# Latent attention on one core: a head's output product moved behind the next head's scores

## The reference

```python
q = (_rms_norm(c_q, q_norm) @ w_q_up).reshape(B, L, H, QK_NOPE + QK_ROPE)   # 128 + 64 per head
q_nope, q_rope = q[..., :QK_NOPE], _rope(q[..., QK_NOPE:], pos)
kv = (_rms_norm(c_kv, kv_norm) @ w_kv_up).reshape(B, L, H, QK_NOPE + V_HEAD)
k_nope, v = kv[..., :QK_NOPE], kv[..., QK_NOPE:]
k_rope = _rope(k_rope, pos)                                                  # one for all heads
for s, e in bounds:                          # 0-16, then blocks of 128 queries
    sc = (q_nope[s:e] . k_nope[:e] + q_rope[s:e] . k_rope[:e]) * scale       # causal
    p = softmax(where(mask, sc, neg))
    outs.append(p @ v[:e])
o = concatenate(outs)
return (o * silu(g)) @ w_out                 # 2048 -> 1024
```

## Time and profile before

| what | value |
|---|---|
| median of three runs | 2272.62 us |
| profiled execution | 2278.24 us |
| its span | 2276.1 us |
| PE busy | 2119.0 us (93%) |
| DVE, ACT, POOL busy | 1245.8, 894.0, 910.9 us |
| the 16 heads (1370.6 to 1665.0 us) | 294.4 us, of which PE busy 281.7 us |
| mean granted clock of TensorE in the heads | 0.98 |

### The profile page before, as it was taken

How to read it: one execution, slowest core, us unless ns; L and a number is a source line. 1 busy time by engine, 2 the same in 40 slices (tenths; PEclk the granted TensorE clock), 3 DMA queues, 4 the chain that set the end, 5 groups by cost and what they waited for, 6 DMA issues and landing times.

```text
span 2276.1 us, 57765 instructions
## 1 busy us (share of the span) xinstructions
PE 2119.0 (93%) x23476; PEld 1799.1 (79%) x23476; DVE 1245.8 (55%) x2016; ACT 894.0 (39%) x2246; POOL 910.9 (40%) x592
## 2 busy tenths in 40 slices
PE   6999999989999999987989999999898999998997
PEld 4789999978888888875989957777698776776775
DVE  8766656665665666664046514545411475428674
ACT  1665555535655555555231123333323101302351
POOL 1132322333133233245437811232344598456455
PEclk8999999999999999997999999999899999999999
DMA  2334444474335334414212211010123221221102
GB/s 96 113 142 157 160 174 168 158 191 78 73 73 96 74 72 96 84 35 142 87 53 93 93 65 38 19 37 19 38 66 130 77 92 56 74 82 57 47 0 74
DMA packets 158991, 198.08 MB, mean 87 GB/s; under 512 B 121040, under 2 KB 123344, under 8 KB 156496
## 3 DMA queue, kind: packets, MB, share of 16 engines
q1 hardware_dynamic: 158800, 195.25, 28.2%
HBM read 156.24 MB, written 38.99 MB: 86 GB/s over the span
## 4 chain that ended last, share of the span: by engine, by line
PE 59%; issue 7%; DVE 5%; POOL 4%; ACT 2%; POOLq 1%; DVEq 0%; ACTq 0%
PE wide L922 9%; PE wide L1416 9%; PE wide L1417 9%; PE wide L1418 9%; PE wide L2059 5%; PE wide L2178 3%; PE wide L1947 2%; PE wide L2132 1%; PE wide L2771 1%; PE wide L2162 1%; PE wide L2451 1%; PE wide L2754 1%; POOL x_w L1221 1%; PE wide L947 1%; PE wide L2136 1%
## 5 line engine op out<-in xcount | busy, mean ns | idle before, releaser
L1416 PE MATMUL wide<-mixed_high,w_high_rwkv_in 128*128 128x264 f32 x880 | 255.1, 290 | 3.6 <-issue 2.1
L1418 PE MATMUL wide<-mixed_high,w_low_rwkv_in 128*128 128x264 f32 x880 | 250.5, 285 | 0.0
L1416 PEld LDWEIGHTS wide<-mixed_high,w_high_rwkv_in 128*128 128x128 f32 x880 | 166.5, 189 | 19.4 <-issue 13.0
L1221 POOL TENSOR_TENSOR x_w<-n,masks 128x192 f32<-128x192 f32 x48 | 28.6, 597 | 357.2 <-ACT n L1094 357.2
L1418 PEld LDWEIGHTS wide<-mixed_high,w_low_rwkv_in 128*128 128x128 f32 x880 | 166.4, 189 | 0.0
L1437 POOL TENSOR_TENSOR w_high<-weights,con 128x1024 fp32r<-128x1024 f32 x45 | 108.7, 2416 | 73.8 <-PE wide L1418 46.3
L644 POOL TENSOR_TENSOR w_low_rwkv_in<-weights,w_high_rwkv_in 128x1024 fp32r<-128x1024 f32 x29 | 70.5, 2431 | 143.9 <-ACT w_high_rwkv_in L477 143.9
L922 PE MATMUL wide<-x_w,n_levels 64*64 64x64 f32 x2752 | 121.4, 223 | 6.4 <-DVE x_w L1173 1.5
L922 PE MATMUL wide<-e,x_w 64*64 64x64 f32 x2752 | 120.2, 219 | 0.7 <-issue 0.7
L1158 DVE TENSOR_TENSOR b_and_k<-wide,b_k_masks 128x384 f32<-128x384 f32 (+1 forms) x160 | 75.3, 512 | 83.0 <-PE wide L982 83.0
L1440 POOL TENSOR_TENSOR w_low<-weights,w_high 128x1024 fp32r<-128x1024 f32 x45 | 118.5, 2632 | 3.5
(11 more groups left out here) (407 smaller groups left out, 6566.2 us busy)
## 6 DMA issues: line engine op xcount, KB each, us to landing
weights<-in_stream SPq DMA_DIRECT2D x200, 512.0 KB, 3.6
forms<-form SPq DMA_DIRECT2D x16, 2020.5 KB, 6.3
forms_in<-forms SPq DMA_DIRECT2D x96, 144.0 KB, 4.6
forms_in<-forms SPq DMA_DIRECT2D x32, 288.0 KB, 4.4
gate_bonus<-forms SPq DMA_DIRECT2D x16, 576.0 KB, 4.3
r_ahat_r<-forms SPq DMA_DIRECT2D x32, 144.0 KB, 3.6
mixed<-gate_bonus SPq DMA_DIRECT2D x14, 264.0 KB, 2.1
gated<-mixed SPq DMA_DIRECT2D x14, 264.0 KB, 4.8
```

The lines of the kernel that those rows point to most:

```text
L1416: pe.matmul(dst, w[0], x[0], start=start, stop=False)
L1418: return pe.matmul(dst, w[1], x[0], start=False, stop=stop)
```

## The change

In all four programs the output product and the gating of head H - 1 are done within head H. On PE, the output product of H - 1 (now the function `pe_output`) follows the scores of H and precedes the projections for H + 1. On DVE, its gating (now `dve_gate`) stands between `share(3)` and the second reciprocal. For head 15 the last output product and gating come at the end, as before.

Two orders within the projections change. When the next head is odd, q comes ahead of k on PE and ACT. When it is even, ACT copies the rotary part after all the exponentials. The wait before the turning moves with it: in front of an odd head it is for the copy of q (which is the fourth of the pair's five copies). The wait for two steps of the rotation, which stood before the output product, goes; the wait for all six steps stays before the scores. The first turn of `over_heads` is written out, and the loop runs the two turns behind it.

The diff:

```diff
--- before.py
+++ after.py
@@ -2066,28 +2066,30 @@
             if x % 2 == 0:
                 ring.wait_full(pe, k_load, j)
                 product(wide[2], wr, 0, Q_TILES).then_inc(e["made"], 1)
-            if not first:
-                pe.wait_ge(e["gated"], 2 * H)
-            mm = product(wide[3], wk, Q_TILES, KV_TILES)
-            mm.then_inc(e["made"] if x % 2 == 0 else ring.done(k_load), 1)
+            def keys():
+                if not first:
+                    pe.wait_ge(e["gated"], 2 * H)
+                mm = product(wide[3], wk, Q_TILES, KV_TILES)
+                mm.then_inc(e["made"] if x % 2 == 0 else ring.done(k_load), 1)
+            if x % 2 == 1:
+                product(wide[2], wq, 0, Q_TILES).then_inc(ring.done(q_load), 1)
+                keys()
+                return
+            keys()
+            ring.wait_full(pe, q_load, j)
             if first:
-                ring.wait_full(pe, q_load, j)
                 pe.wait_ge(e["evac"], 1)
                 for b in range(2):
                     mm = pe.matmul(wide[1][:, b, 0:HALF], mcon("rot_mla", P), q_rope_raw[:, b * HALF:(b + 1) * HALF], start=True, stop=True)
                 mm.then_inc(e["made"], 1)
                 product(wide[2], wq, 0, Q_TILES).then_inc(e["made"], 1)
                 return
-            if x % 2 == 0:
-                ring.wait_full(pe, q_load, j)
-                pe.wait_ge(e["evac"], 5 * pair + 1)
-            mm = product(wide[2], wq, 0, Q_TILES)
-            mm.then_inc(e["made"] if x % 2 == 0 else ring.done(q_load), 1)
-            if x % 2 == 0:
-                pe.wait_ge(e["evac"], 5 * pair + 2)
-                for b in range(2):
-                    mm = pe.matmul(wide[3][:, b, 0:HALF], mcon("rot_mla", P), q_rope_raw[:, b * HALF:(b + 1) * HALF], start=True, stop=True)
-                mm.then_inc(e["made"], 1)
+            pe.wait_ge(e["evac"], 5 * pair + 1)
+            product(wide[2], wq, 0, Q_TILES).then_inc(e["made"], 1)
+            pe.wait_ge(e["evac"], 5 * pair + 2)
+            for b in range(2):
+                mm = pe.matmul(wide[3][:, b, 0:HALF], mcon("rot_mla", P), q_rope_raw[:, b * HALF:(b + 1) * HALF], start=True, stop=True)
+            mm.then_inc(e["made"], 1)
 
         def act_up(act, x, j, what, first=False):
 
@@ -2141,14 +2143,15 @@
                 pe.matmul(dst, q_nope[:, queries], k_nope[:, keys], start=True, stop=False)
                 mm = pe.matmul(dst, own[:, queries], k_rope_upper[:, keys], start=False, stop=True)
             mm.then_inc(e["scores"], 1)
+            if not (isinstance(H, int) and H == 0):
+                pe_output(pe, H - 1, (x - 1) % 2, wide[3])
             if not ends:
                 pe_up(pe, H + 1, (x + 1) % PER_TURN, j + (x + 1) // PER_TURN)
                 pair_next = pair + (x % 2)
-                pe.wait_ge(e["evac"], 5 * pair_next + (3 if x % 2 else 5))
+                pe.wait_ge(e["evac"], 5 * pair_next + (3 if x % 2 else 4))
             else:
                 pe_out_begin(pe, H)
                 pe.wait_ge(e["pt"], 6 * H + 6)
-            pv = wide[1] if ends else wide[3]
 
             for n, (kb, q0, q1, col, bank, piece) in enumerate(TURNED):
                 if n == 0:
@@ -2162,20 +2165,20 @@
                     mm = pe.transpose(wide[2][0:size(kb), bank, at:at + size(t)], p_of(t, Q_EDGES[kb], Q_EDGES[kb + 1]), ident[0:size(t), 0:size(t)])
                 if n in (0, 2, 3, 5):
                     mm.then_inc(e["turned"], 1)
+            if ends:
+                pe.wait_ge(e["gated"], 2 * H + 2)
+                pe_output(pe, H, x % 2, wide[1])
+
+        def pe_output(pe, H, slot, pv):
 
             pe.wait_ge(e["v_now"], 2 * H + 2)
-            if not ends:
-                if x % 2:
-                    pe.wait_ge(e["rope"], 6 * pair_next + 2)
-            else:
-                pe.wait_ge(e["gated"], 2 * H + 2)
             cut = Q_EDGES[3]
             for kb, done in ((0, 2), (2, 3), (1, 4), (3, 5), (4, 6)):
                 pe.wait_ge(e["pt"], 6 * H + 6 + done)
                 for b, (lo, hi) in enumerate(((0, cut), (cut, L))):
                     seen_from = max(lo, Q_EDGES[kb])
                     if seen_from < hi:
-                        mm = pe.matmul(pv[:, b, seen_from - lo:hi - lo], v_now[0:size(kb), x % 2, kb, :],
+                        mm = pe.matmul(pv[:, b, seen_from - lo:hi - lo], v_now[0:size(kb), slot, kb, :],
                                        probs_t[0:size(kb), kb, seen_from:hi], start=kb == 0, stop=kb == (1, 4)[b])
             mm.then_inc(e["pv"], 1)
 
@@ -2204,13 +2207,11 @@
 
             soften(4, 5)
             soften(3, 5)
-            if not ends and nx % 2 == 0:
-                act_up(act, nx, nj, 0)
             for t in (2, 1, 0):
                 soften(t, 12)
             if not ends:
-                act_up(act, nx, nj, 1)
-                act_up(act, nx, nj, 2)
+                for what in (0, 1, 2) if nx % 2 == 0 else (2, 1):
+                    act_up(act, nx, nj, what)
 
             for n, (kb, q0, q1, col, bank, piece) in enumerate(TURNED):
                 act.wait_ge(e["turned"], 4 * H + piece + 1)
@@ -2261,6 +2262,8 @@
             after(13)
             share(4)
             share(3)
+            if not (isinstance(H, int) and H == 0):
+                dve_gate(dve, H - 1, wide[3])
             dve.wait_ge(e["exp"], Q_BLOCKS * H + 5)
             step(dve.reciprocal(row_sum[:, 0:3], row_sum[:, 0:3]))
             after(16)
@@ -2270,12 +2273,17 @@
             if not ends and x % 2:
                 dve_rope(dve, j + (x + 1) // PER_TURN, (x + 1) % PER_TURN)
 
+            if ends:
+                dve_gate(dve, H, wide[1])
+
+        def dve_gate(dve, H, pv):
+
             dve.wait_ge(e["pv"], H + 2)
             flat = z_t[:].rearrange("p k n -> p (k n)")
             cut = Q_EDGES[3]
             for b, (lo, hi) in enumerate(((0, cut), (cut, L))):
                 at = flat[:, bass.ds(H * L + lo, hi - lo)]
-                dve.scalar_tensor_tensor(at, (wide[1] if ends else wide[3])[:, b, 0:hi - lo], 0.5, at, ALU.mult, ALU.mult).then_inc(e["gated"], 1)
+                dve.scalar_tensor_tensor(at, pv[:, b, 0:hi - lo], 0.5, at, ALU.mult, ALU.mult).then_inc(e["gated"], 1)
 
         def pool_v(pool, H, slot):
 
@@ -2317,7 +2325,9 @@
                 pool_split_head(pool, H, lambda n: y_lo[:].rearrange("p k n -> p (k n)")[:, bass.ds(n * L, L)])
 
         def over_heads(eng, body):
-            with eng.Fori(0, HEADS // PER_TURN - 1) as j:
+            for x in range(PER_TURN):
+                body(eng, 0, x, False)
+            with eng.Fori(1, HEADS // PER_TURN - 1) as j:
                 for x in range(PER_TURN):
                     body(eng, j, x, False)
             for x in range(PER_TURN):
```

## The result

| | before | after |
|---|---|---|
| median | 2271.68 us (4 runs) | 2284.68 us (4 runs) |
| the same, timed again with the changed kernel (19 and 8 runs) | 2276.28 us | 2285.41 us |
| profiled execution | 2278.24 us | 2281.89 us |
| from the first scores to output product 15 | 289.04 us | 295.00 us |

The change makes the kernel slower: ratio 1.0056, 95% interval 1.0038 to 1.0073, and 1.0038 (1.0025 to 1.0051) in the second comparison. My likeliest case was within 0.2%, 4.5 us; the measured difference lies outside it. The time lies in the stated range (2265 to 2286). The profile after happens to be of one of its faster executions, and the one of before of a slower one, so the two differ by 3.65 us only. The heads are compared by themselves, from profile to profile.

The account below looks back on a forecast made before the run. PE was taken to set the pace; -4.6 - 5.5 + 11.1 - 2.5 - 3.0 + 2.7 + 1.7 + 3.4 = +3.3 us gave 2281.5 profiled, 2275.9 as median. Its own range was 2272 to 2280, over the cases 2265 to 2286.

Parts of the forecast that it names:

- Part 1: Output product behind the next scores: no more waiting of about 0.3 us for ACT in 15 products, -4.6 us.
- Part 2: q ahead of k in short heads: idle 0.78 us for ACT's copy of q goes in seven heads, -5.5 us.
- Part 3: Scores right behind the turning in long heads: seven new idle times of 1.59 us for the rotation's additions, +11.1 us.
- Part 4: DVE shares 2, 1, 0 beside POOL's pieces end later but before the turning: nothing, at worst +0.15 x 6.
- rival E: POOL delays the short heads too, shares ending near 13.5 us: +4.8 on the sum, 2280.7 us; chance 0.06.
- Part 5: Head 14: idle before the turning 2.9 instead of 5.4 us, -2.5; shorter clock fall, -4.7 + 1.7 = -3.0.
- Part 6: Head 15: first output projection waits for head 14's gating, +2.7 us, and a clock fall behind it, +1.7.
- Part 7: Clock at the seven rotation waits: two falls of seven, 1.7 us each, +3.4; bounds 0 and +11.9.
- B: Clock falls at six or seven of the seven rotation waits: +10 to +17 in all, 2283 to 2290 us; chance 0.25.
- C: Transposes don't hold up the clock, so it falls at all seven waits for two stretches: +23.7, 2296 us; chance 0.04.
- D: Faster: DVE keeps ahead of POOL's pieces in heads 14 and 15, no clock fall: -7.3, 2265.3 us; chance 0.17.

Follow-up runs that it names:

- e8: Changed kernel with one wait for all six turned pieces ahead of the output product in place of five between its matmuls: 2282.72 us, 1.0018 against before.
- e2: Kernel before with only q put ahead of k where the next head is odd: 2271.28 us, 0.9985 against before.
- e3: Changed kernel with k ahead of q again where the next head is odd: 2297.09 us, 1.0100 against before.
- e1: Changed kernel, but the scores of even heads wait for the first two rotation additions and not all four: 2266.95 us, 0.9970 against before.
- c1: The changed kernel without an edit, timed again: 2285.41 us, 1.0038 against before.
- e4: Changed kernel with POOL's four output-weight pieces put ahead of the wait for output product 13: 2276.41 us, 1.0007 against before.
- e7: Changed kernel with one more DVE multiplication ahead of the rotation's additions, seven times, lengthening PE's idle time: 2289.63 us, 1.0051 against before.
- e5: Changed kernel with the gating of the head before moved from between the shares to behind share 0: 2286.83 us, 1.0041 against before.

## Why the prediction was right or wrong

The mechanism of the forecast was right: the rotation eats the gain. Its size was short by 6 to 10 us, which put the likeliest case (+3.3, within 0.2%) on the wrong side of the line. By its own parts, in the heads of the two profiles, start to start:

- **Part 1, the output product, wrong.** -4.6 us was for five waits on ACT. The product still takes 3.36 us (1462.17 to 1465.53). From the scores to the projections it adds 3.45 us in long heads and 3.52 to 3.55 in short ones, in place of the 3.36 taken out behind the turning, +2.3 over the 15 products. The step from turning to scores, which the bound allowed for, is 0.1 us shorter in eight heads than that from turning to product: -0.8. So +1.5 in place of -4.6. e8 shows that its pace is its own. The step that failed is "it takes 3.36, so it waits about 0.3 us for ACT": a difference from another line's pace was read as a wait, where no row named ACT. The term is off by 6.1 us, the largest miss.
- **Part 2, q ahead of k, right, a little more than forecast.** From the projections to the turning a short head takes 5.34 us in place of 6.28 (6.20 in head 12): seven times 0.9, -6.5, as in e2, against -5.5. That the swap also covers the gating wait (e3) was said for the changed order only.
- **Part 3, the rotation, right.** Turning start to scores 3.84 to 4.00 us where 3.93 was forecast; +11.0 us in seven heads against +11.1. e1 takes it away.
- **Part 4, right.** Shares 2, 1, 0 took 1.75 us where DVE came first and 2.81 where POOL did, and delayed no short head; rival E did not occur.
- **Part 5, head 14, right in sum.** Idle 2.78 us (2.9 forecast) with a fall of 3.4 us. It cost 1.0 us instead of 1.7 (turning to scores 3.28 us against 2.25). Idle -2.6 and clock -4.7 + 1.0: -6.3 against -5.5.
- **Part 6, head 15, too high.** The wait is 1.29 us, not 2.7, at the lower bound: of both biases only one was held up (0.98 us), the other took 0.17. No fall followed, so +1.3 in place of +4.4.
- **Part 7, the clock, too low.** Three falls at the seven waits and not two: +5.0 against +3.4.

The parts as measured: +2.3 - 0.8 - 6.5 + 11.0 - 6.3 + 1.3 + 5.0 = +6.0; the heads differ by 5.96. That the forecast of +3.3 came as near as this to the heads is in part luck: two misses, parts 1 and 6, were 6.1 and 3.1 us and of opposite sign.

The median is +9.1 (second comparison, interval +5.7 to +11.6) to +13.0 (first, +8.6 to +16.6). The heads' +6 lies inside the second interval and not inside the first, and what lies between is open. It does not show outside the heads: the span less the heads is 1987 us in the profile before and 1985 and 1988 in the two of the changed kernel, among 1983 to 1995 over all the kernels. Inside the heads the falls can differ from one execution to the next. c1 has the same three as the first profile, but e4, whose program is the same up to head 12, has none in front of head 4.

Part 7 rested on a reading that does not hold: 2.04 us was not the shortest idle time with a fall behind it. In the first mixer of the kernel before PE idles 0.74, 0.72 and 0.65 us between short matmuls from 1015 to 1020 us, at a clock of 1.00 and 0.99, and then:

```profile
1020.90:1024.10 3.20, 3.20 (x76) 3.20 (x74) 2.97 (x5) 0.53 (x4) 1.94 (x1) 0.50 0.00 0
```

The rivals: the forecast said that the third fall decides (+5.0 by its sum), and there were three. B as it was stated (a fall at six or seven of the waits, +10 to +17) gave a time that the first comparison meets, but not by its mechanism: three of seven fell. C falls: four of the seven waits, each with the transposes ahead of it, had no fall behind them, and no fall there lasted two stretches. D did not occur. On the Trainium skill's rule for the shared port pair (SBUF — State Buffer), that whichever of the two starts first holds the other up for its whole instruction: this case's trace agrees. In head 14 POOL's piece started 0.05 us ahead of the share, and the three shares took 7.04 us past three pieces; in head 6 the share started 0.08 us ahead, and POOL's piece took 1.44 us in place of 1.30.

## What to carry to other kernels

Before moving work out from between two others, ask what it covered there: the 3.4 us of the output product hid the end of another engine's chain. The scores needed only the first half of it, so the remedy was the number in the wait and not the order. Move work behind other work only where something arrives late; here that was one head of sixteen, and moving POOL's four pieces away from it cured most of that. And a stretch that is slower than another line's pace is no wait until a row names who was waited for.

## What the runs showed of the hardware

- Idle times of TensorE of the same length had different sequels: 1.44 us with a clock of 0.50 behind it and 1.44 with 1.00, in one execution; 2.14 likewise (e7); 2.78 us before turning 14 with 0.50 behind it in the changed kernel, 2.77 in e1 and 2.78 in e8 without a fall. Three of seven fell with 1.44 to 1.59 us, in front of heads 4, 8 and 12 or (e8) 6, 10 and 14, two of seven in e3 and e4, three of seven with 2.11 to 2.24, and none of seven with no wait (e1). A fall of 3.4 us cost a short head 1.6 to 1.7 us (17.05 against 15.36).
- Three `tensor_scalar` in a row that take 0.70 us alone took 1.75 to 2.86 us beside POOL's pieces of 1.3 us, and 7.04 to 7.70 beside pieces of 2.35 us. DVE's multiplication, maxima and gating, which read PSUM, were not slowed: beside a POOL piece the rotation's multiplication took 0.71 us (e4), the maximum over 528 columns 0.71 (head 15), the gating 0.75 (e5).
- The output product of 1,808 columns took 3.36 us whether its inputs were just made or long made, with five waits or one.
